# One-layer hybrid decoder step: the chunk's triangular inverse keeps its transposed copy by VectorE 32x32 transposes instead of TensorE products

## The chip, the cores and the metric

The kernel runs on one core of a Trainium2 chip, in one launch. The metric is the device time of that launch in microseconds (us). PE is TensorE, DVE is VectorE, ACT is ScalarE, POOL is GpSimd, and SP is SyncE, which only issues transfers here.

## What is computed

One layer of a decoder is applied to a prompt of 16 + 1024 rows and to 8 single-row samples: RMSNorm, an input projection, RWKV-7 time mixing beside forgetting attention, gates, an output projection and an MLP. The change lies inside the time mixing of the prompt. In the reference it is a recurrence over rows for each of 8 heads:

```python
def step(state, inp):
    r_t, w_t, k_t, v_t, kk_t, a_t = inp
    s_kk = jnp.einsum('bhvk,bhk->bhv', state, kk_t)
    state = (state * w_t[:, :, None, :]
             - s_kk[..., None] * (kk_t * a_t)[:, :, None, :]
             + v_t[..., None] * k_t[:, :, None, :])
    return state, jnp.einsum('bhvk,bhk->bhv', state, r_t)
```

The kernel computes it for 104 rows at a time (a chunk). Within a chunk the terms `s_kk` of later rows depend on earlier ones, which gives a unit triangular 104x104 system for each head, and its inverse is what the change touches.

## The kernel before

The 1040 prompt rows are 10 chunks (`c` = 0 to 9), which run one after the other; each engine has its own program for a chunk (`pe_chunk` L996, `act_chunk` L1532, `dve_chunk` L1884, the loop of POOL L2316), and they meet through counting semaphores. Each list `Steps` (L597 to L610) names an engine's steps in order, and `wait(steps, name)` waits for one of them.

**Fillers.** The chunk's own matrix products are small and depend on each other, so TensorE fills its waiting time with the next projection of the layer. A unit of it is 3 matmuls of 128x128 by 350 columns (L384 to L386; in chunk 0 one fp32 matmul, L388). A chunk has 48 units: 24 of weight tile 0, then 24 of weight tile 1. `fill.run(n)` puts n units at a fixed place of the program: 16 at the chunk's start, 4 among the first products, 4 ahead of the inverse (so that it begins with tile 1), 2 in each of levels 1 to 6, 4 behind, 8 at the end. The first unit of a tile waits until ScalarE has rounded its weights (`fill_split_high`) and VectorE has made the remainder (`fill_split_low`, L585 to L590, two instructions of 128x512 for tile 1).

**The inverse.** Heads lie as 8 blocks of columns; of the 104 rows, 64 are "top" and 40 "low", two separate triangles held in one tile at 64 columns a head. The inverse grows by levels: at level lv diagonal blocks of 2^lv are joined to blocks of twice the size by X <- X - X B X, with B the products masked for this level. X is kept as `Xm`, and its transpose as `XTr`, since a matmul wants its left operand transposed. Heads go in two halves, q = 0 and 1. `by_halves` (L1015) issues one head as two fp32 matmuls, 64x64 (L1020) and 40x40 (L1021); the profile shows each as two records. The steps are:

- POOL makes the mask products `bm_lv_top` (64x512) and `bm_lv_low` (40x320) at L2326 for levels 0 to 5, alternately in two buffers, from the step `mask_b1` on.
- VectorE, behind the mask products of L1913, does `fill_split_low` (L1918), waits for `bm_0_low` and makes `XTr` = I - B (`xt_init`, L1920).
- TensorE turns it into `Xm` (steps `x_0`, `x_1`, L1068 to L1071), and ScalarE copies that from PSUM (L1565 to L1567).
- In a level TensorE makes `t1` = B X (L1073 to L1082), ScalarE copies it (L1575), 2 filler units run, then TensorE makes `t2x` (L1084 to L1095) and `t2` (L1096 to L1099). VectorE subtracts `t2x` from `Xm` (L1934) and `t2` from `XTr` (L1940). The next `t1` waits for the first, the next `t2x` for the second.
- Level 5 puts its `XTr` part into `XTF` (L1943, L1945), and level 6 joins top and low (L1106, L1115, L1948).

```python
for q in range(2):
    for j in range(4):
        last = by_halves(4 + q, j, T1, XTr, 4 * q + j)
    ch_pe.done(last, f"t2_{lv}_{q}")
```

Of the kernel before, what the change touches and what calls it, by code (L numbers as in the profile page):

```python
# [41 lines left out]
P = 128  # L42
# [7 lines left out]
C = 104  # L50
NC = TP // C
HD = 64
NH = 8
# [12 lines left out]
C_LV = C_CM + 2 * C  # L66
N_LV = 7
# [64 lines left out]
def build(nc, A):  # L132
    with ExitStack() as ctx:
        def sem(name):
            return ctx.enter_context(nc.semaphore(name))
# [449 lines left out]
        def fill_split_low(dve, i, s):  # L585

            dve.wait_ge(wf_high[s], i)
            for k0, k1, t in WF[s]:
# [5 lines left out]
        LEVELS = range(1, N_LV)  # L594
        ch_pe = Steps(sem("ch_pe"), ["nat_k", "nat_b", "nat_v"]
                      + [f"prod_{m}{i}" for i in range(2) for m in "kb"] + ["z", "x_0", "x_1"]
                      + [f"{t}_{lv}_{q}" for lv in LEVELS for t in (("t1", "t2x", "t2") if lv < N_LV - 1 else ("t1", "t2"))  # L597
                         for q in range(2)]
                      + ["u", "y", "s", "yt"])
        ch_act = Steps(sem("ch_act"), ["v", "e1", "e3", "e2", "nat_k", "z", "x_0", "x_1"]  # L600
# [3 lines left out]
                       + [f"mask_{m}{i}" for i in range(2) for m in "kb"] + ["xt_init"]  # L604
# [5 lines left out]
        ch_pool = Steps(sem("ch_pool"), [f"bm_{lv}_{b}" for lv in range(N_LV - 1) for b in ("top", "low")] + ["bonus", "gate"])  # L610
# [279 lines left out]
        def _(pe):  # L890
# [105 lines left out]
            def pe_chunk(c):  # L996
                fill = Filler(pe, c + V_FOX0, NS, hl_made if c == 1 else None) if c else fill0

                def wait(steps, name):
                    pe.wait_ge(steps.sem, steps.after(c, name))  # L1000
# [66 lines left out]
                wait(ch_dve, "xt_init")  # L1067
                for q in range(2):  # L1068
                    for j in range(4):
                        last = by_halves(q, j, XTr, identP)  # L1070
                    ch_pe.done(last, f"x_{q}")  # L1071
                for lv in LEVELS[:-1]:
                    for q in range(2):  # L1073
                        if q == 0:
                            pe.wait_ge(ch_pool.sem, ch_pool.after(c, f"bm_{lv}_low"))
                        if lv == 1:
                            wait(ch_act, f"x_{q}")
                        else:
                            wait(ch_dve, f"x_{lv - 1}_{q}_x")
                        for j in range(4):  # L1080
                            last = by_halves(q, j, Bm[lv % 2], Xm, 4 * q + j)
                        ch_pe.done(last, f"t1_{lv}_{q}")  # L1082
                    fill.run(2)
                    for q in range(2):  # L1084
                        wait(ch_act, f"t1_{lv}_{q}")
                        if lv > 1:
                            wait(ch_dve, f"x_{lv - 1}_{q}_xt")
                        for j in range(4):
                            h = 4 * q + j
                            if lv < N_LV - 2:  # L1090
                                last = by_halves(2 + q, j, XTr, T1, h)
                            else:
                                last = pe.matmul(PS[top, 2 + q, j * HB:(j + 1) * HB], XTr[top, h], T1[top, h],
                                                 start=True, stop=True)
                        ch_pe.done(last, f"t2x_{lv}_{q}")  # L1095
                    for q in range(2):  # L1096
                        for j in range(4):
                            last = by_halves(4 + q, j, T1, XTr, 4 * q + j)
                        ch_pe.done(last, f"t2_{lv}_{q}")  # L1099
# [354 lines left out]
        def _(act):  # L1454
# [77 lines left out]
            def act_chunk(c, gates, early=True):  # L1532
# [32 lines left out]
                for q in range(2):  # L1565
                    wait(ch_pe, f"x_{q}")
                    ch_act.done(act.copy(quad(Xm, q), PS[0:C, q, 0:4 * HB]), f"x_{q}")  # L1567
                out(2)
                for lv in LEVELS:
                    for q in range(2):  # L1570
                        wait(ch_pe, f"t1_{lv}_{q}")
                        if lv > 1:
                            wait(ch_pe, f"t2_{lv - 1}_{q}")
                        part = slice(0, C) if lv < N_LV - 1 else low
                        ch_act.done(act.copy(quad(T1, q)[part], PS[part, q, 0:4 * HB]), f"t1_{lv}_{q}")  # L1575
# [210 lines left out]
        def _(dve):  # L1786
# [93 lines left out]
            order(dve.memset(XTF[low, :, top], 0.0))  # L1880
            order(dve.tensor_copy(identP[top], ident[top, 0:HB]))
            order(dve.tensor_copy(identP[low], ident[low, HB:2 * HB]))
            dve.sem_inc(ch_dve.sem, 1)
            def dve_chunk(c, early=True):  # L1884
# [25 lines left out]
                for i in range(2):  # L1910
                    for m, dst, bank in (("k", MK, 4), ("b", MB, 0)):
# [4 lines left out]
                            cm, ALU.mult), f"mask_{m}{i}")  # L1916
                if early:
                    fill_split_low(dve, c, 1)  # L1918
                wait(ch_pool, "bm_0_low")
                done(dve.tensor_tensor(XTr[0:C], identP[0:C].unsqueeze(1).to_broadcast([C, NH, HB]),  # L1920
                                       Bm[0][0:C], ALU.subtract), "xt_init")
# [4 lines left out]
                for lv in LEVELS:  # L1926
# [9 lines left out]
                    for q in range(2):  # L1936
                        wait(ch_pe, f"t2_{lv}_{q}")
                        four = slice(4 * q, 4 * q + 4)
                        if lv < N_LV - 2:
                            done(dve.tensor_tensor(quad(XTr, q), quad(XTr, q), PS[0:C, 4 + q, 0:4 * HB],  # L1940
                                                   ALU.subtract), f"x_{lv}_{q}_xt")
                        elif lv < N_LV - 1:
# [370 lines left out]
        def _(pool):  # L2313

            pool.sem_inc(ch_pool.sem, 1)
            with pool.Fori(0, NC) as c:  # L2316
                pool.wait_ge(ch_dve.sem, ch_dve.after(c, "mask_b1"))
                for lv in range(N_LV - 1):
                    if lv == 2:
                        pool.wait_ge(ch_dve.sem, ch_dve.after(c, "xt_init"))  # L2320
# [154 lines left out]
```

## Time and profile before

| | us |
|---|---|
| median of 3 runs (2086.79 to 2089.35) | 2087.89 |
| the profiled execution, its own time | 2083.8 |
| its span, first to last instruction | 2082.0 |
| PE busy in it | 2001.7 (96%) |
| DVE, ACT, POOL busy | 953.7, 631.4, 219.9 |

The ten chunks begin at 232.6, 300.6, 358.3, 415.8, 473.3, 530.8, 588.2, 645.7, 703.2 and 760.7 us of the span, and the last one's own products end at 806.2. Times in the rows are counted from the start of the span. Chunk 5 (530.76 to 588.24) stands for chunks 1 to 9, which repeat to 0.3 us.

### The profile page before, as it was taken

Reading aid. Unit: us, or ns where it says so; the run is one execution under the profiler, and the core shown is the slowest. Engines: PE = TensorE matmul, PEld = TensorE weight load, DVE = VectorE, ACT = ScalarE, POOL = GpSimd, SP = SyncE. Lnnn points to the kernel's source line nnn. Section 1 sums busy time; section 2 is a strip of 40 time slices with the busy share of each in tenths; the row PEclk is TensorE's granted clock in tenths of the full one; section 3 lists DMA queues with packets and bytes.
Section 4 is the critical chain, followed back from the end, with each engine's and each line's share of the span. In section 5 each row is a group of like instructions: output and inputs, shape, how many; then the busy total and the mean of one; then the engine's idle time right before and its main releaser. Section 6 shows DMA issues by size and latency. Waiting matters only on the chain.

```text
span 2082.0 us, 43790 instructions
## 1 busy us (share of the span) xinstructions
PE 2001.7 (96%) x18026; PEld 1864.0 (90%) x18026; DVE 953.7 (46%) x1509; ACT 631.4 (30%) x1011; POOL 219.9 (11%) x197
## 2 busy tenths in 40 slices
PE   7999999999999998798998999999999999999997
PEld 7997679999999998785666999999999999999997
DVE  6556564445555554417786654332132223222324
ACT  5114333322333333135455543321022012102313
POOL 0000212323333321121110000000000000000000
PEclk9999999999999999999999999999999999999998
DMA  4213721122223213657643741111111111111112
GB/s 172 90 32 137 241 48 41 42 59 50 60 70 80 80 55 94 178 189 240 236 162 138 243 146 41 51 41 51 41 50 41 51 40 50 40 50 41 50 41 83
DMA packets 111982, 189.65 MB, mean 91 GB/s; under 512 B 62870, under 2 KB 66230, under 8 KB 110406
## 3 DMA queue, kind: packets, MB, share of 16 engines
q1 hardware_dynamic: 109542, 179.15, 27.5%
q10 hardware_dynamic: 2304, 8.50, 1.3%
q8 instruction: 109, 1.79, 0.4%
q14 instruction: 27, 0.22, 0.0%
HBM read 149.83 MB, written 37.79 MB: 90 GB/s over the span
## 4 chain that ended last, share of the span: by engine, by line
PE 52%; issue 31%; POOL 7%; DMA 3%; DVE 3%; SPq 2%; ACT 1%; POOLq 0%; ACTq 0%; DVEq 0%
PE ps L294 44%; POOL arena L2326 6%; PE ps L384 1%; DMA weights<-in_wu 1%; PE ps L385 1%; PE ps L386 1%; SPq L811 1%; SPq L817 1%; DMA normed<-in_vp 1%; DMA normed<-in_kp 1%; PE ps L1272 1%; PE ps L1213 1%; DVE arena L2085 1%; DVE arena L2104 1%; POOL arena L2332 1%
## 5 line engine op out<-in xcount | busy, mean ns | idle before, releaser
L294 PE MATMUL ps<-h_high,wb_split 128*128 128x350 f32 (+1 forms) x1536 | 290.6, 324 | 0.0
L294 PE MATMUL ps<-ff_high,wb_split 128*128 128x350 f32 x1488 | 280.2, 323 | 0.0
L304 ACT CAST wb_split<-weights 128x1024 fp32r<-128x1024 f32 x88 | 92.2, 1047 | 592.9 <-PE ps L294 592.9
L294 PEld LDWEIGHTS ps<-h_high,wb_split 128*128 128x128 f32 x1536 | 254.5, 189 | 0.4
L294 PEld LDWEIGHTS ps<-ff_high,wb_split 128*128 128x128 f32 x1488 | 246.7, 189 | 0.0
L2243 DVE TENSOR_TENSOR arena<-arena,ps 128x1050 f32 (+1 forms) x39 | 48.7, 1249 | 311.1 <-PE ps L294 311.1
L2326 POOL TENSOR_TENSOR arena<-arena,constants 64x512 f32<-64x512 f32 x120 | 140.6, 1172 | 357.7 <-DVE arena L1913 322.4
L1020 PEld LDWEIGHTS ps<-arena 64*64 64x64 f32 x2400 | 145.0, 135 | 21.2 <-issue 10.0
L1020 PE MATMUL ps<-arena 64*64 64x64 f32 x2400 | 154.0, 219 | 7.6 <-POOL arena L2326 7.5
L294 PE MATMUL ps<-ff_low,wb_split 128*128 128x350 f32 x744 | 160.6, 324 | 0.0
L386 PE MATMUL ps<-fill_high,w_fill_low 128*128 128x350 f32 x468 | 152.9, 327 | 0.0
L1021 PE MATMUL ps<-arena 40*40 40x64 f32 x2400 | 149.6, 218 | 0.0
L2260 DVE SCALAR_TENSOR_TENSOR squares<-ps,arena 128x1050 f32<-128x1050 f32 x32 | 40.1, 1252 | 220.2 <-PE ps L294 209.8
L1021 PEld LDWEIGHTS ps<-arena 40*40 40x40 f32 x2400 | 138.7, 112 | 0.0
L294 PEld LDWEIGHTS ps<-ff_low,wb_split 128*128 128x128 f32 x744 | 127.0, 189 | 0.0
L294 PE MATMUL ps<-h_high,w_split 128*128 128x350 f32 (+1 forms) x576 | 115.2, 332 | 2.9 <-DVE w_split L308 2.9
L308 DVE TENSOR_TENSOR wb_split<-weights,wb_split 128x1024 fp32r<-128x1024 f32 x88 | 107.3, 1219 | 2.3 <-DVE fox L2222 1.8
L1934 DVE TENSOR_TENSOR arena<-arena,ps 104x256 f32<-104x256 f32 (+1 forms) x100 | 42.0, 420 | 142.7 <-PE ps L1021 117.6
L385 PE MATMUL ps<-fill_low,w_fill 128*128 128x350 f32 x312 | 103.2, 331 | 0.0
L294 PEld LDWEIGHTS ps<-h_high,w_split 128*128 128x128 f32 x576 | 97.5, 191 | 5.7 <-DVE w_split L308 3.2
L384 PE MATMUL ps<-fill_high,w_fill 128*128 128x350 f32 x234 | 82.7, 353 | 12.3 <-POOL w_fill_low L589 9.0
L386 PEld LDWEIGHTS ps<-fill_high,w_fill_low 128*128 128x128 f32 x468 | 90.1, 193 | 0.0
(346 smaller groups left out, 3672.0 us busy)
## 6 DMA issues: line engine op xcount, KB each, us to landing
weights<-in_wu SPq DMA_DIRECT2D x122, 512.0 KB, 3.7
normed<-in_vp SPq DMA_DIRECT2D x64, 260.0 KB, 4.7
normed<-in_kp SPq DMA_DIRECT2D x64, 256.0 KB, 4.6
arena<-chunk_dram SPq DMA_DIRECT2D x10, 1248.0 KB, 6.9
arena<-gate_dram SPq DMA_DIRECT2D x16, 525.0 KB, 4.2
chunk_dram<-arena SPq DMA_DIRECT2D x12, 520.0 KB, 5.0
chunk_dram<-fox SPq DMA_DIRECT2D x12, 520.0 KB, 4.6
arena<-samp_dram SPq DMA_DIRECT2D x10, 512.0 KB, 10.1
```

What stands on the lines that cost most here:

```text
L294: last = pe.matmul(PS[:, 3 * s + g, 0:n], ws[s][wh][:, k * P:(k + 1) * P], tile_of(x[xh], k)[:, g * G:g * G + n], start=(k == 0 and wh + x ...
L304: act.copy(of[0][s][0], W[:, s]).then_inc(w_hi[s], 1)
L308: dve.tensor_tensor(of[0][s][1], W[:, s], of[0][s][0], ALU.subtract).then_inc(w_split[s], 1)
L384: self.pe.matmul(out, fill_w(s, k), HF[k][:, at], start=(i == 0), stop=False)
L385: self.pe.matmul(out, fill_w(s, k), HL[:, k, at], start=False, stop=False)
L386: last = self.pe.matmul(out, wl_, HF[k][:, at], start=False, stop=(i == KT - 1))
L1020: pe.matmul(PS[top, bank, at], a[top], b[top], start=True, stop=True)
L1021: return pe.matmul(PS[low, bank, at], a[low, 0:HR], b[low], start=True, stop=True)
L1934: done(dve.tensor_tensor(quad(Xm, q)[part], quad(Xm, q)[part], PS[part, 2 + q, 0:4 * HB], ALU.subtract), f"x_{lv}_{q}_x")
L2243: dve.tensor_tensor(dst, dst, grp(s), ALU.add).then_inc(evac[s], 1)
L2260: dve.scalar_tensor_tensor(g3(RL[s]), grp(s), 0.0, rstd1, ALU.max, ALU.mult)\
L2326: ch_pool.done(pool.tensor_tensor(Bm[lv % 2][part, :, 0:n], MB[part, :, 0, part], mask.unsqueeze(1).to_broadcast([n, NH, n]), ALU.mult), f ...
```

## The change

The transposed copy `XTr` is no longer made by products up to block size 32: VectorE turns 32x32 blocks of `Xm` into it (`blocks_turned`), which is enough while X has no entries outside diagonal blocks of 32. The product `t2` is left for level 5 (and 6). The start works the other way round: VectorE makes the level-0 mask product itself (two instructions), then `XTr`, then `Xm` by one transpose of 128x512, so that the steps `x_0` and `x_1` of TensorE and ScalarE are gone. `fill_split_low` comes behind that. POOL begins with level 1. The fillers of levels 1 to 5 are 0, 3, 2, 3, 2 units instead of 2 each, the same 10 in all. ScalarE's copy of `t1` waits for `t2x` of the level before. Two more memsets stand ahead of chunk 0.

```diff
--- before.py
+++ after.py
@@ -592,22 +592,24 @@
         bonus_added = sem("bonus_added")
 
         LEVELS = range(1, N_LV)
+        IN_LEVEL = (0, 3, 2, 3, 2)
         ch_pe = Steps(sem("ch_pe"), ["nat_k", "nat_b", "nat_v"]
-                      + [f"prod_{m}{i}" for i in range(2) for m in "kb"] + ["z", "x_0", "x_1"]
-                      + [f"{t}_{lv}_{q}" for lv in LEVELS for t in (("t1", "t2x", "t2") if lv < N_LV - 1 else ("t1", "t2"))
+                      + [f"prod_{m}{i}" for i in range(2) for m in "kb"] + ["z"]
+                      + [f"{t}_{lv}_{q}" for lv in LEVELS for t in ("t1", *(("t2x",) if lv < N_LV - 1 else ()),
+                                                                    *(("t2",) if lv >= N_LV - 2 else ()))
                          for q in range(2)]
                       + ["u", "y", "s", "yt"])
-        ch_act = Steps(sem("ch_act"), ["v", "e1", "e3", "e2", "nat_k", "z", "x_0", "x_1"]
+        ch_act = Steps(sem("ch_act"), ["v", "e1", "e3", "e2", "nat_k", "z"]
                        + [f"t1_{lv}_{q}" for lv in LEVELS for q in range(2)]
                        + ["nu", "ln", "rstd"] + [f"y_{p}" for p in range(HP)])
         ch_dve = Steps(sem("ch_dve"), [f"scan_{p}" for p in range(HP)] + ["lm", "r", "k", "b", "a", "nat_b", "nat_v"]
-                       + [f"mask_{m}{i}" for i in range(2) for m in "kb"] + ["xt_init"]
+                       + [f"mask_{m}{i}" for i in range(2) for m in "kb"] + ["bm_0_top", "bm_0_low", "xt_init", "x_init"]
                        + [f"x_{lv}_{q}_{t}" for lv in LEVELS
                           for t, q in (([("x", 0), ("x", 1)] if lv < N_LV - 1 else [])
                                        + [(t, q) for q in range(2)
                                           for t in (("xt", "xl") if lv == N_LV - 2 else ("xt",))])]
                        + ["sum", "mean", "state_sum", "state", "center", "sq", "var", "norm"])
-        ch_pool = Steps(sem("ch_pool"), [f"bm_{lv}_{b}" for lv in range(N_LV - 1) for b in ("top", "low")] + ["bonus", "gate"])
+        ch_pool = Steps(sem("ch_pool"), [f"bm_{lv}_{b}" for lv in LEVELS[:-1] for b in ("top", "low")] + ["bonus", "gate"])
 
         ds_pe, ds_act, ds_dve = sem("ds_pe"), sem("ds_act"), sem("ds_dve")
         ds_store, ds_load = sem("ds_store"), sem("ds_load")
@@ -1064,23 +1066,18 @@
                                      skip_group_check=True)
                 ch_pe.done(last, "z")
                 fill.run(4)
-                wait(ch_dve, "xt_init")
-                for q in range(2):
-                    for j in range(4):
-                        last = by_halves(q, j, XTr, identP)
-                    ch_pe.done(last, f"x_{q}")
+                wait(ch_dve, "x_init")
                 for lv in LEVELS[:-1]:
                     for q in range(2):
                         if q == 0:
                             pe.wait_ge(ch_pool.sem, ch_pool.after(c, f"bm_{lv}_low"))
-                        if lv == 1:
-                            wait(ch_act, f"x_{q}")
-                        else:
+                        if lv > 1:
                             wait(ch_dve, f"x_{lv - 1}_{q}_x")
                         for j in range(4):
                             last = by_halves(q, j, Bm[lv % 2], Xm, 4 * q + j)
                         ch_pe.done(last, f"t1_{lv}_{q}")
-                    fill.run(2)
+                    if IN_LEVEL[lv - 1]:
+                        fill.run(IN_LEVEL[lv - 1])
                     for q in range(2):
                         wait(ch_act, f"t1_{lv}_{q}")
                         if lv > 1:
@@ -1093,10 +1090,10 @@
                                 last = pe.matmul(PS[top, 2 + q, j * HB:(j + 1) * HB], XTr[top, h], T1[top, h],
                                                  start=True, stop=True)
                         ch_pe.done(last, f"t2x_{lv}_{q}")
-                    for q in range(2):
-                        for j in range(4):
-                            last = by_halves(4 + q, j, T1, XTr, 4 * q + j)
-                        ch_pe.done(last, f"t2_{lv}_{q}")
+                for q in range(2):
+                    for j in range(4):
+                        last = by_halves(4 + q, j, T1, XTr, 4 * q + j)
+                    ch_pe.done(last, f"t2_{N_LV - 2}_{q}")
 
                 lv = N_LV - 1
                 for q in range(2):
@@ -1562,15 +1559,12 @@
                 def quad(ap, q):
                     return ap[0:C, 4 * q:4 * q + 4].rearrange("p a b -> p (a b)")
 
-                for q in range(2):
-                    wait(ch_pe, f"x_{q}")
-                    ch_act.done(act.copy(quad(Xm, q), PS[0:C, q, 0:4 * HB]), f"x_{q}")
                 out(2)
                 for lv in LEVELS:
                     for q in range(2):
                         wait(ch_pe, f"t1_{lv}_{q}")
                         if lv > 1:
-                            wait(ch_pe, f"t2_{lv - 1}_{q}")
+                            wait(ch_pe, f"{'t2x' if lv < N_LV - 1 else 't2'}_{lv - 1}_{q}")
                         part = slice(0, C) if lv < N_LV - 1 else low
                         ch_act.done(act.copy(quad(T1, q)[part], PS[part, q, 0:4 * HB]), f"t1_{lv}_{q}")
                     if lv == 4:
@@ -1878,6 +1872,8 @@
             for b in Bm:
                 order(dve.memset(b[low, :, HR:HB], 0.0))
             order(dve.memset(XTF[low, :, top], 0.0))
+            order(dve.memset(XTr, 0.0))
+            order(dve.memset(Xm[96:P], 0.0))
             order(dve.tensor_copy(identP[top], ident[top, 0:HB]))
             order(dve.tensor_copy(identP[low], ident[low, HB:2 * HB]))
             dve.sem_inc(ch_dve.sem, 1)
@@ -1914,11 +1910,20 @@
                             dst[0:C].rearrange("p (e a) x t -> p e a (x t)", e=2)[:, :, 2 * i:2 * i + 2],
                             PS[0:C, bank:bank + 2, 0:4 * C].rearrange("p e (a n) -> p e a n", a=2),
                             cm, ALU.mult), f"mask_{m}{i}")
+                for part, name in ((top, "top"), (low, "low")):
+                    n = part.stop - part.start
+                    mask = cst[part, C_LV + part.start:C_LV + part.stop]
+                    done(dve.tensor_tensor(XTr[part, :, 0:n], MB[part, :, 0, part],
+                                           mask.unsqueeze(1).to_broadcast([n, NH, n]), ALU.mult), f"bm_0_{name}")
+                done(dve.tensor_tensor(XTr[0:C], identP[0:C].unsqueeze(1).to_broadcast([C, NH, HB]),
+                                       XTr[0:C], ALU.subtract), "xt_init")
+
+                def blocks_turned(dst, src):
+                    return dve.transpose(dst.rearrange("p a b -> p (a b)"), src.rearrange("p a b -> p (a b)"))
+
+                done(blocks_turned(Xm, XTr), "x_init")
                 if early:
                     fill_split_low(dve, c, 1)
-                wait(ch_pool, "bm_0_low")
-                done(dve.tensor_tensor(XTr[0:C], identP[0:C].unsqueeze(1).to_broadcast([C, NH, HB]),
-                                       Bm[0][0:C], ALU.subtract), "xt_init")
 
                 def quad(ap, q):
                     return ap[0:C, 4 * q:4 * q + 4].rearrange("p a b -> p (a b)")
@@ -1934,12 +1939,12 @@
                             done(dve.tensor_tensor(quad(Xm, q)[part], quad(Xm, q)[part], PS[part, 2 + q, 0:4 * HB],
                                                    ALU.subtract), f"x_{lv}_{q}_x")
                     for q in range(2):
-                        wait(ch_pe, f"t2_{lv}_{q}")
                         four = slice(4 * q, 4 * q + 4)
                         if lv < N_LV - 2:
-                            done(dve.tensor_tensor(quad(XTr, q), quad(XTr, q), PS[0:C, 4 + q, 0:4 * HB],
-                                                   ALU.subtract), f"x_{lv}_{q}_xt")
-                        elif lv < N_LV - 1:
+                            done(blocks_turned(XTr[:, four], Xm[:, four]), f"x_{lv}_{q}_xt")
+                            continue
+                        wait(ch_pe, f"t2_{lv}_{q}")
+                        if lv < N_LV - 1:
                             done(dve.tensor_tensor(XTF[top, four, top], XTr[top, four], moved(4 + q, top, HB),
                                                    ALU.subtract), f"x_{lv}_{q}_xt")
                             done(dve.tensor_tensor(XTF[low, four, low], XTr[low, four, 0:HR], moved(4 + q, low, HR),
@@ -2315,9 +2320,7 @@
             pool.sem_inc(ch_pool.sem, 1)
             with pool.Fori(0, NC) as c:
                 pool.wait_ge(ch_dve.sem, ch_dve.after(c, "mask_b1"))
-                for lv in range(N_LV - 1):
-                    if lv == 2:
-                        pool.wait_ge(ch_dve.sem, ch_dve.after(c, "xt_init"))
+                for lv in LEVELS[:-1]:
                     if lv > 2:
                         pool.wait_ge(ch_pe.sem, ch_pe.after(c, f"t1_{lv - 2}_1"))
                     for part, name in ((top, "top"), (low, "low")):
```

## Rows read from the trace of the kernel before

**Rows 1.** Page: busy time, and the PE and clock lines of 40 slices

```profile
PE 2001.7 (96%) x18026; PEld 1864.0 (90%) x18026; DVE 953.7 (46%) x1509; ACT 631.4 (30%) x1011; POOL 219.9 (11%) x197
...
PE   7999999999999998798998999999999999999997
...
PEclk9999999999999999999999999999999999999998
```

**Rows 2.** Stages of chunk 5: busy time, granted clock, DMA share, GB/s

```profile
core 0: us, PE busy (x) PEld busy (x) DVE busy (x) ACT busy (x) POOL busy (x), PEclk, DMA share, GB/s
546.29:550.38 4.09, 4.09 (x103) 3.81 (x102) 1.69 (x4) 0.74 (x2) 3.19 (x4) 1.00 0.24 34
...
542.00:546.29 4.29, 3.45 (x71) 2.95 (x70) 0.00 (x0) 1.84 (x5) 3.98 (x4) 1.00 0.09 8
...
530.76:588.24 57.48, 56.64 (x850) 53.04 (x849) 29.78 (x52) 17.61 (x38) 16.48 (x14) 1.00 0.22 54
```

**Rows 3.** Timeline of PE in chunk 5: start, us, instruction, [idle before <-releaser]

```profile
542.08 0.27 PE L1020 MATMUL ps<-arena 64*64 64x64 f32 x1
...
544.07 0.27 PE L1020 MATMUL ps<-arena 64*64 64x64 f32 x1 [0.84 <-POOL arena L2326]
...
545.14 0.43 PE L384 MATMUL ps<-fill_high_b,w_fill1b 128*128 128x350 f32 x1
...
546.29 0.27 PE L1020 MATMUL ps<-arena 64*64 64x64 f32 x1
...
549.23 0.43 PE L384 MATMUL ps<-fill_high,w_fill1b 128*128 128x350 f32 x1
...
562.66 0.27 PE L1093 MATMUL ps<-arena 64*64 64x64 f32 x1
```

**Rows 4.** Timeline of ACT and DVE in level 1 of chunk 5

```profile
544.79 0.37 ACT L1575 COPY arena<-ps 104x256 f32<-104x256 f32 x1 [0.80 <-PE ps L1021]
...
547.09 0.42 DVE L1934 TENSOR_TENSOR arena<-arena,ps 104x256 f32<-104x256 f32 x1 [5.15 <-PE ps L1021]
```

**Rows 5.** Timeline of DVE ahead of the inverse of chunk 5

```profile
535.98 2.08 DVE L1913 TENSOR_TENSOR arena<-ps,constants 104x832 f32<-104x832 f32 x2 [0.55 <-PE ps L1051]
538.10 0.69 DVE L589 TENSOR_TENSOR w_fill_low<-weights,w_fill1a 128x512 fp32r<-128x512 f32 x1
538.71 1.76 DVE L589 TENSOR_TENSOR w_fill_low<-weights,w_fill1b 128x512 fp32r<-128x512 f32 x1
541.25 0.69 DVE L1920 TENSOR_TENSOR arena<-arena 104x512 f32<-104x512 f32 x1 [0.79 <-POOL arena L2326]
```

**Rows 6.** Timeline of POOL there: levels 0 and 1, and level 2's first

```profile
538.14 1.77 POOL L2326 TENSOR_TENSOR arena<-arena,constants 64x512 f32<-64x512 f32 x1 [8.99 <-DVE arena L1913]
539.99 1.23 POOL L2326 TENSOR_TENSOR arena<-arena,constants 40x320 f32<-40x320 f32 x1
541.29 1.78 POOL L2326 TENSOR_TENSOR arena<-arena,constants 64x512 f32<-64x512 f32 x1
543.15 0.86 POOL L2326 TENSOR_TENSOR arena<-arena,constants 40x320 f32<-40x320 f32 x1
544.17 1.26 POOL L2326 TENSOR_TENSOR arena<-arena,constants 64x512 f32<-64x512 f32 x1 [0.16 <-POOL arena L2326]
```

**Rows 7.** Groups by line over the ten chunks, PE

```profile
L1020 PE MATMUL ps<-arena 64*64 64x64 f32 x2400 | 154.0, 219 | 7.6 <-POOL arena L2326 7.5
L1021 PE MATMUL ps<-arena 40*40 40x64 f32 x2400 | 149.6, 218 | 0.0
```

**Rows 8.** Timeline of DVE ahead of chunk 0

```profile
225.82 0.27 DVE L1877 MEMSET arena<- 128x256 f32 x1 [0.17 <-DVE arena L1860]
...
226.90 0.48 DVE L1880 MEMSET arena<- 40x512 f32 x1 [0.17 <-DVE arena L1879]
...
229.05 1.60 DVE L1895 TENSOR_TENSOR_SCAN arena<-constants,arena 128x104 f32<-128x104 f32 x4 [1.22 <-DMA arena<-chunk_dram]
```

**Rows 9.** Waits of chunks 1 to 9: engine, line, releaser: us in total, times, longest

```profile
DVE arena L1895 <- PE ps L993: 6.3, 8, 0.8
```

## The prediction

> **What bounds the kernel now.** I read the page first: TensorE is busy 96% of the span and its clock is granted at full speed (2.4 GHz) in nearly every slice [rows 1]. The change lies only in the ten chunks, so the next view is the table of stages. In chunk 5, TensorE is busy 56.64 of 57.48 us, DVE 29.78, ACT 17.61, POOL 16.48, and the DMA share is 0.22 [rows 2]. A busy TensorE that runs small dependent products may still be waiting inside, so I looked at the timeline: records follow each other without a gap, except 0.84 us in front of level 1, which POOL's mask product ends [rows 3]. Over all chunks these gaps are 7.5 us [rows 7]. So a chunk lasts as long as TensorE's own program, and a product that goes away is worth its time, unless something that it covered becomes visible. DVE's next chunk begins when TensorE releases it, not when a DMA does [rows 9], so no transfer sets the period. 0.2% of the time, 4.2 us, is about what a measurement of this kernel can tell from no change.
>
> **The removed products.** From 546.29 to 549.23 TensorE does three product steps of 8 heads (t2x, t2 and the next t1), then turns to a filler [rows 3]. From 544.07 to 545.14 it does one, 1.07 us. Two more steps cost 2.94 - 1.07 = 1.87, so a step is 0.94 us and the turn to a filler 0.13. The four t2 of levels 1 to 4 are 4 x 0.94 = **3.76 us** a chunk. One block of fillers fewer (level 1 has none; the units are the same) saves one turn, **0.13**. The step from the first product x_0 to level 1's first product lasts 544.07 - 542.08 = **1.99 us**, its wait for POOL and its ScalarE copies within it, and all of it goes. As a check on the count: 40 of 120 heads' products of L1020 and L1021 a chunk go, which in [rows 7] is 800 of 2400 records on each line.
>
> **What comes in place of the x steps.** DVE now makes Xm before level 1 may start. Its mask products end at 535.98 + 2.08 = 538.06 [rows 5]. Then come the top mask product (64x512: by L1920's 512 columns, 0.69), the low one (40x320), xt_init (0.69) and the transpose of 512 columns, while POOL starts level 1's masks at 538.14 as before. They get in each other's way. The second L589 takes 1.76 against 0.69 for the first, and it ends 0.56 after POOL's first product at 539.91; POOL's 64x512 takes 1.77 and 1.78 beside DVE and 1.26 alone [rows 5, 6]. So each stands still until the other's instruction ends, and then needs 0.56 (DVE, 512 columns), 1.13 (POOL, 512) or 0.75 (POOL, 320: 540.47 to 541.22). Walked through: top to 538.79; POOL to 539.91; low to 540.27 (320 of 512 columns of 0.56); POOL to 541.02, which is level 1's mask, long before need; xt_init to 541.58; the transpose to 542.31 if it costs 0.69; released after 0.06, which is what POOL's end at 543.15 + 0.86 = 544.01 needs to reach TensorE at 544.07 [rows 3, 6]. TensorE arrives at 542.08 and so waits **0.29 us**.
>
> The rows don't show either whether a transpose beside POOL stands still. In the walk POOL would be in level 2's top product until 542.71, and a transpose that waits for it ends at 543.27, 0.96 later than I have it. The rows show a block only between two operations that both read two SBUF tensors, while L1934, with one operand in SBUF and one in PSUM, costs its 0.42 in a stage where POOL is busy for 3.19 of 4.09 us [rows 2, 4]. So I take the free one. The Trainium skill ("SBUF — State Buffer", section Who interferes with whom) says that only VectorE operations with two SBUF inputs, or in a two-port mode, exclude GpSimd, and lists fp32 copies, but not transposes, among the latter. By the first half of that rule the sum would stay; if a transpose counts as a copy, it would lose 10 us over the chunks.
>
> **Level 1.** t1 is followed at once by t2x, which needs ScalarE's copy: it ends 544.79 + 0.37 - 544.07 = 1.09 after t1's start [rows 4], plus 0.06 release is 1.15, against 0.94 of work: **0.21 lost**. Then DVE has fill_split_low in front of the x update. By the same walk its halves end at 543.27 (behind POOL's top product) and 544.58 (behind its low one), while the update is wanted at 542.37 + 1.15 + 0.80 = 544.32 (0.80 is t2x's start to DVE's start, 546.29 to 547.09 [rows 3, 4]): **0.30 lost**. The filler that needs the split comes in level 2, behind the next t1, at about 546.1, so it doesn't wait. Without a filler in level 1 that cover is not missed either.
>
> **The turnaround.** Before, t2 ran while DVE updated Xm. Now the next t1 follows t2x. It can start at 0.80 + 0.42 + 0.06 = 1.28 after t2x's start, against 0.94 of work: 0.34 lost in each of four levels, **1.36 us**. Half q = 1 is just in time (0.46 later, like the products). A transpose of XTr costs TensorE nothing: in a level with two filler units it has from the Xm updates' end (0.41 after t1's start) until t1 and the fillers are over, 1.07 + 1.15 - 0.41 = 1.8 us for the first half (1.15 is the two fillers, 545.14 to 546.29) and 0.47 more for the second, against 0.42 and 0.84. POOL's masks lie a level ahead and start earlier than before. ScalarE has two copies less. The memsets ahead of chunk 0 (about 0.5 each, [rows 8]) fit in the 1.22 us that DVE waits there for its DMA. Loads of weights hang on the same units as before and have whole levels of time.
>
> **The sum.** 3.76 + 0.13 + 1.99 - 0.29 - 0.21 - 0.30 - 1.36 = 3.72 us a chunk, 37 us for ten (chunk 0 has no split behind x_init, but other fillers; I count it alike). What follows the chunks hangs on TensorE too and moves up as a whole. Against the profiled execution's 2083.8 that gives 2047; the median of the runs lies 4 us above it, so I say **2051**.
>
> **Rivals.**
> 1. *Dearer hand-overs* (0.07). Each new wait of TensorE is a two-engine hand-over, priced above from waits that were hidden. If x_init is late by 1.3 more (a dear transpose that also waits for POOL) and each of five hand-overs costs 0.25 more, 1.2 us a chunk is left: 2076. For it: DVE and POOL do collide there [rows 5, 6]. Against: the 0.06 of the one visible release.
> 2. *Slower: the transposes are so slow that TensorE waits for them in each level* (0.04). With a cost of T for 256 columns, x_init takes 2T, and the second half's transpose is late in the levels with two fillers from T = 1.1, with three from T = 1.3. The losses eat up the 3.72 at about T = 1.4, 3.3 times an L1934; at T = 1.8 a chunk is 4 us longer and the time is 2127. Against it: nothing on DVE costs over half of that per column.
> 3. *Nothing becomes visible* (0.05): DVE and ScalarE answer within the running half, and the whole 5.9 us of a chunk go: 2029. Against it: 0.80 and 0.42 are measured and t1 can't start without Xm.
> 4. *The time is not TensorE's* (0.03): the chunk's period is held by a transfer or by DVE's own chain, and what is saved comes back as a wait at the chunk's start: no change, 2088. Against it: [rows 2, 9].
> That the short waits lower the clock is no rival with a price: the stage with the 0.84 us gap has a granted clock of 1.00 [rows 2].
>
> **How the numbers follow.** The forecast has 0.81. Its own bounds: without collisions and without the split's delay a chunk saves 4.3, with a turnaround also 0.1 shorter 4.7, so 2040; with the transpose blocked (0.96) or dear, and hand-overs 0.1 dearer, it saves about 2.2, so 2066. The four rivals, 0.19, lie outside. Faster by over 0.2% are the forecast and rivals 1 and 3: 0.93; no change 0.03; slower 0.04.
>
> **What would show it.** In the profile after: L1020 with 1600 records instead of 2400; chunk periods of 53.8 instead of 57.48; a wait of about 0.3 in front of level 1 with DVE's transpose as releaser and none by POOL; gaps of about 0.34 in front of t1 in levels 2 to 5, released by L1934, with somewhat more in level 2; transposes of 0.42 (256 columns) and 0.69 (512). Gaps in front of t2x in levels 2 to 5 would speak for rival 2, a gap at a chunk's start for rival 4. I am wrong in the mechanism if the period shrinks by less than 2 us while the gaps are as small as I say.

## The result, and the profile after

Four runs of the changed kernel have a median of 2051.8 us (2047.5 to 2055.8), four of the kernel before 2087.3 (2085.7 to 2089.4): ratio of the two 0.9831, 95% interval 0.9811 to 0.9851. The forecast was 2051, within 2040 to 2066. The profiled execution took 2047.5 us against 2083.8.

The page of the changed kernel, its head, its clock line, and the groups of the two lines of 8-head products (before: [rows 1, 7]; L1022 and L1023 are the old L1020 and L1021, L1939 the old L1934, L2329 the old L2326, and L1922 is the transpose):

```profile
span 2045.6 us, 40598 instructions
...
PE 1963.2 (96%) x16426; PEld 1820.4 (89%) x16426; DVE 987.8 (48%) x1541; ACT 625.9 (31%) x991; POOL 202.3 (10%) x177
...
PEclk9999999999999998999999999999999999999999
...
L1022 PE MATMUL ps<-arena 64*64 64x64 f32 x1600 | 113.0, 220 | 9.7 <-DVE arena L1939 5.3
...
L1023 PE MATMUL ps<-arena 40*40 40x64 f32 x1600 | 109.2, 218 | 0.0
```

800 records have gone from each line, TensorE is busy 38.5 us less and VectorE 34.1 more, and the wait in front of the products is now VectorE's work, not POOL's. The idle total that is printed there has hardly grown (9.7 us against 7.6).

The table of stages for chunk 5, first the whole chunk, then level 1 to level 2's t1, then level 2's t2x to level 3's. The columns are those of [rows 2]: stretch, length, busy time of PE, PEld (loading of weights), DVE, ACT and POOL, granted clock, DMA share and GB/s.

```profile
512.23:565.78 53.55, 52.60 (x689) 48.63 (x688) 33.09 (x55) 16.99 (x36) 14.58 (x12) 1.00 0.23 58
523.84:526.48 2.64, 2.28 (x65) 2.03 (x65) 2.52 (x4) 1.19 (x3) 2.40 (x3) 1.00 0.10 5
529.18:532.69 3.51, 3.35 (x71) 2.96 (x70) 1.74 (x4) 0.74 (x2) 2.21 (x3) 1.00 0.43 149
```

A chunk lasts 53.55 us in place of 57.48, 3.93 less; chunks 2 to 8 agree to 0.06 us, chunk 1 went from 57.72 to 53.76 and chunk 0 from 68.01 to 64.56. The timeline of TensorE there (before: [rows 3]):

```profile
523.84 0.27 PE L1022 MATMUL ps<-arena 64*64 64x64 f32 x1
...
526.48 0.24 PE L1022 MATMUL ps<-arena 64*64 64x64 f32 x1 [0.35 <-DVE arena L1939]
...
529.18 0.27 PE L1022 MATMUL ps<-arena 64*64 64x64 f32 x1
...
530.47 0.24 PE L1022 MATMUL ps<-arena 64*64 64x64 f32 x1 [0.15 <-POOL arena L2329]
...
540.20 0.27 PE L1090 MATMUL ps<-arena 64*64 64x64 f32 x1
```

Counted from the chunk's start, level 1 begins at 523.84 - 512.23 = 11.61 (before 13.31) and level 5's t2x at 27.97 (before 31.90). From level 2's t2x at 529.18 to the next t1 it is 1.29. The idle time printed there is only 0.15, because it is counted from the modelled end of the last product; the start-to-start time is what a level pays. POOL is named as its releaser, but its mask for this level had ended at 528.1; what ended at 530.47 is the next level's. VectorE's L1939, over at 530.33, is what TensorE waited for.

In front of level 1 the PE timeline prints no idle time, but the one of the weight loads does, with VectorE's transpose as the releaser:

```profile
523.83 0.13 PEld L1022 LDWEIGHTS ps<-arena 64*64 64x64 f32 x1 [0.41 <-DVE arena L1922]
```

The fillers in front of level 1 begin at 9.28 of the chunk (before 9.21) and take 2.11 where nothing waits behind them, so TensorE arrives at 11.39 and waits 0.22.

The timeline of VectorE ahead of the inverse, and POOL's instructions at the time of xt_init and of the transpose (before: [rows 5, 6]):

```profile
519.58 2.16 DVE L1916 TENSOR_TENSOR arena<-arena,constants 64x512 f32<-64x512 f32 x2
521.78 1.25 DVE L1918 TENSOR_TENSOR arena<-arena 104x512 f32<-104x512 f32 x1
523.07 0.71 DVE L1922 STREAM_TRANSPOSE arena<-arena 128x512 f32<-128x512 f32 x1
523.82 0.91 DVE L589 TENSOR_TENSOR w_fill_low<-weights,w_fill1a 128x512 fp32r<-128x512 f32 x1
524.65 1.35 DVE L589 TENSOR_TENSOR w_fill_low<-weights,w_fill1b 128x512 fp32r<-128x512 f32 x1
525.93 0.95 DVE L1939 TENSOR_TENSOR arena<-arena,ps 104x256 f32<-104x256 f32 x2
526.91 0.93 DVE L1922 STREAM_TRANSPOSE arena<-arena 128x256 f32<-128x256 f32 x2
```

```profile
521.47 1.01 POOL L2329 TENSOR_TENSOR arena<-arena,constants 40x320 f32<-40x320 f32 x1
522.56 1.61 POOL L2329 TENSOR_TENSOR arena<-arena,constants 64x512 f32<-64x512 f32 x1
```

xt_init (L1918) costs 1.25 in place of 0.69 because POOL holds it up, as walked through: it ends 0.55 after POOL's 40x320. The transpose from 523.07 runs its 0.71 in the middle of a POOL instruction (522.56 to 524.17) and isn't held up. Nor is any other, by the view of its line (the durations are the shortest, the median and the longest in ns), though 40 of the 90 overlap an instruction of POOL:

```profile
L1922 DVE STREAM_TRANSPOSE arena<-arena x90: 445/445/712, 244.6 to 753.2; 128x256 f32<-128x256 f32 x80, 128x512 f32<-128x512 f32 x10
```

### The profile page after: what moved, and what is told of

The parts are those of the page before. It is cut to its first block, busy times and chain, and to the rows that moved or that the text cites. A ratio compares the mean times of both kernels' runs of the same rounds, so it can differ in the third digit from the quotient of the medians.

```text
span 2045.6 us, 40598 instructions
## 1 busy us (share of the span) xinstructions
PE 1963.2 (96%) x16426; PEld 1820.4 (89%) x16426; DVE 987.8 (48%) x1541; ACT 625.9 (31%) x991; POOL 202.3 (10%) x177
## 4 chain that ended last, share of the span: by engine, by line
PE 53%; issue 31%; POOL 7%; DVE 3%; DMA 2%; SPq 2%; ACT 1%; POOLq 0%; ACTq 0%; DVEq 0%
PE ps L294 44%; POOL arena L2329 6%; PE ps L384 1%; PE ps L386 1%; PE ps L385 1%; SPq L819 1%; DMA normed<-in_vp 1%; POOL w_fill_low L589 1%; PE ps L1210 1%; DMA weights<-in_wu 1%; DMA normed<-in_kp 1%; PE ps L1269 1%; DVE arena L2109 1%; DVE arena L2090 1%; PE ps L1314 1%
## 5 line engine op out<-in xcount | busy, mean ns | idle before, releaser
L2329 POOL TENSOR_TENSOR arena<-arena,constants 64x512 f32<-64x512 f32 x100 | 122.0, 1220 | 344.7 <-DVE arena L1909 323.2
L1022 PEld LDWEIGHTS ps<-arena 64*64 64x64 f32 x1600 | 101.0, 134 | 25.9 <-issue 17.0
L1022 PE MATMUL ps<-arena 64*64 64x64 f32 x1600 | 113.0, 220 | 9.7 <-DVE arena L1939 5.3
L1023 PE MATMUL ps<-arena 40*40 40x64 f32 x1600 | 109.2, 218 | 0.0
L1023 PEld LDWEIGHTS ps<-arena 40*40 40x40 f32 x1600 | 93.6, 112 | 0.0
L2090 DVE CUSTOM_DVE_ANT_0 arena<-ps,arena 104x416 f32<-104x416 f32 (+3 forms) x152 | 68.1, 494 | 31.8 <-PE ps L1314 31.7
```

The lines of the kernel that those rows point to most:

```text
L1022: pe.matmul(PS[top, bank, at], a[top], b[top], start=True, stop=True)
L1023: return pe.matmul(PS[low, bank, at], a[low, 0:HR], b[low], start=True, stop=True)
L2090: dve.tensor_tensor_reduce(Sm[u % 3][0:C, e, lo:hi].rearrange("p b t -> p (b t)"), PS[0:C, 2 * (n % 2) + e, (lo - CUTS[c][0]) * C:(hi - CU ...
L2329: ch_pool.done(pool.tensor_tensor(Bm[lv % 2][part, :, 0:n], MB[part, :, 0, part], mask.unsqueeze(1).to_broadcast([n, NH, n]), ALU.mult), f ...
```

## The experiments

Where the outcome is a chunk period, it is that of chunk 5 in the table of stages.

**The changed kernel again.** 

> The changed kernel once more, in more rounds beside the kernel before, since its four runs lay 8 us apart. If the chunks alone carry the change, the ratio is 0.982 to 0.984 (2083.8 less 36 us) and the chunk period is again 53.55 us. If part of it was chance in the stages behind the chunks, where the two profiled executions differ by 1.3 us of waits, the ratio moves by up to 0.001 with the same period.

Median 2051.0 (five runs), ratio 0.9835, interval 0.9813 to 0.9858; period 53.54. The ratio holds. The runs still spread over 6 us. From the last product of the last chunk to the end it took 1276.1 us in the profile of before, 1277.7 in that of the changed kernel and 1281.2 in this one, with nothing changed there: this spread comes from the stages behind the chunks, so below the periods decide, which repeat to some 0.03 us.

**Only the levels.** Made from the kernel before: the start as it was, two fillers in each level. ScalarE's copy of `t1` waits for `t2x`, and the two memsets are there, as in the changed kernel.

```diff
-                    for q in range(2):
-                        for j in range(4):
-                            last = by_halves(4 + q, j, T1, XTr, 4 * q + j)
-                        ch_pe.done(last, f"t2_{lv}_{q}")
+                for q in range(2):
+                    for j in range(4):
+                        last = by_halves(4 + q, j, T1, XTr, 4 * q + j)
+                    ch_pe.done(last, f"t2_{N_LV - 2}_{q}")
...
-                            done(dve.tensor_tensor(quad(XTr, q), quad(XTr, q), PS[0:C, 4 + q, 0:4 * HB],
-                                                   ALU.subtract), f"x_{lv}_{q}_xt")
+                            done(blocks_turned(XTr[:, four], Xm[:, four]), f"x_{lv}_{q}_xt")
```

> Only the levels are changed: XTr by transposes in levels 1 to 4; the start (POOL's level-0 mask, x_0 and x_1 by TensorE) and two filler units in each level as before. Theory (a chunk lasts as long as TensorE's program): four steps of 0.94 us less, four turnarounds of 0.34 more, 2.40 us a chunk: period 55.1, 24 us in all, ratio 0.9885. Rival (the t2 products only filled time in which TensorE waits for Xm, and the gain sits in the start): under 1 us a chunk, period 56.5 or more, ratio 0.995 or more.

```profile
518.98:574.18 55.20, 53.81 (x722) 49.62 (x721) 29.94 (x52) 17.61 (x38) 16.48 (x14) 1.00 0.22 56
```

2.28 us a chunk less (2.40 expected), ratio 0.9893 (0.9867 to 0.9919). The rival falls: the four t2 steps were worth their time less the turnaround. The wait for POOL in front of level 1 stays, 0.77 here.

**Only the start.** Made from the changed kernel: t2 is a product in all levels, TensorE makes it within each level, and ScalarE's copy waits for it again.

```diff
-                            done(blocks_turned(XTr[:, four], Xm[:, four]), f"x_{lv}_{q}_xt")
-                            continue
+                            done(dve.tensor_tensor(quad(XTr, q), quad(XTr, q), PS[0:C, 4 + q, 0:4 * HB],
+                                                   ALU.subtract), f"x_{lv}_{q}_xt")
```

> Only the start is changed: VectorE makes the level-0 mask product, XTr and, by one transpose, Xm; t2 is a TensorE product again in all levels; fillers 0, 3, 2, 3, 2 as in the changed kernel. Theory: 1.70 us less up to level 1, 0.21 lost in front of level 1's t2x, 0.13 for a filler block less: 1.6 us a chunk, period 55.9, 16 us, ratio 0.992. Together with the levels alone this should make the whole, 3.9 us. Rival (the gain sits in the start): 3 us or more a chunk, period 54.5, ratio 0.986.

```profile
521.85:577.57 55.72, 55.58 (x818) 52.05 (x816) 32.88 (x55) 16.96 (x36) 14.56 (x12) 1.00 0.23 56
```

1.76 us a chunk less (1.70 - 0.21 + 0.13 = 1.62 expected), ratio 0.9918 (0.9893 to 0.9942). The parts add up within 0.11: 2.28 + 1.76 = 4.04 against 3.93 for both. Only in the whole does TensorE wait for an update of Xm that stands behind fill_split_low, about 0.2 (1.49 from level 1's t2x to level 2's t1 against 1.30 in the later levels).

**Even fillers.** `IN_LEVEL = (2, 2, 2, 2, 2)` in the changed kernel. 

> The changed kernel with two filler units in each of levels 1 to 5, as before the change. Theory: level 1's first unit is of weight tile 1 and waits for fill_split_low, which VectorE now ends 13.8 us after the chunk's start (12.7 would be in time), so level 1 grows and levels 2 and 4 shrink by a unit each: 1.0 us a chunk more than the changed kernel, period 54.6, with a gap of about 1.1 in front of level 1's filler. Rival (the order of the fillers is of no account, TensorE is busy anyway): period 53.5 to 53.7.

```profile
518.20:572.83 54.63, 52.80 (x689) 48.62 (x688) 33.19 (x55) 16.96 (x36) 14.54 (x12) 1.00 0.22 57
```

The timeline of TensorE has the gap where it was expected:

```profile
532.03 0.43 PE L384 MATMUL ps<-fill_high_b,w_fill1b 128*128 128x350 f32 x1 [1.07 <-DVE w_fill_low L589]
```

So moving level 1's fillers away is a needed part of the change, worth 1.08 us a chunk once fill_split_low comes late (ratio 0.9892).

**The split first.** In the changed kernel `fill_split_low(dve, c, 1)` moves from behind x_init to ahead of the level-0 mask product. 

> The changed kernel with fill_split_low back in its old place, ahead of VectorE's level-0 mask product. Theory (POOL and VectorE block each other for whole instructions when both read two SBUF tensors): x_init is there at 14.6 us of the chunk in place of 11.5, level 2 no longer waits for VectorE, period 56.3. Rival (no blocking, only VectorE's own 2.4 us of split and less): the split would cost 1.3 us at most, since without blocking its halves take 0.69 each: period 54.9 or less.

x_init came when the blocking says it does: TensorE starts at 14.57 us of the chunk (14.6 expected). Here is VectorE in chunk 5 behind the split (the level-0 mask product in its two instructions, xt_init, the transpose), and the first product of level 1:

```profile
540.15 2.85 DVE L1918 TENSOR_TENSOR arena<-arena,constants 64x512 f32<-64x512 f32 x2
543.03 1.24 DVE L1920 TENSOR_TENSOR arena<-arena 104x512 f32<-104x512 f32 x1
544.30 0.71 DVE L1924 STREAM_TRANSPOSE arena<-arena 128x512 f32<-128x512 f32 x1
```

```profile
545.07 0.27 PE L1022 MATMUL ps<-arena 64*64 64x64 f32 x1 [3.08 <-DVE arena L1924]
```

But the periods are 57.3 to 59.8, not 56.3, and the ratio is 1.0014 (1.0000 to 1.0029). The stages of chunk 6: the wait for x_init, the products of level 1 to level 2's t1, the three fillers, and what follows:

```profile
600.00:602.57 2.57, 0.00 (x1) 0.00 (x1) 2.44 (x3) 0.00 (x0) 1.14 (x2) 0.78 0.12 7
602.57:607.95 5.38, 5.38 (x97) 5.26 (x97) 1.74 (x4) 1.12 (x3) 2.12 (x2) 0.50 0.60 173
607.95:611.00 3.05, 3.05 (x13) 2.67 (x15) 0.00 (x0) 0.37 (x1) 2.13 (x2) 0.50 0.13 54
611.00:616.00 5.00, 4.69 (x103) 4.19 (x101) 2.18 (x6) 0.75 (x2) 2.14 (x2) 0.93 0.01 3
```

After the wait of 3.1 us the granted clock is 0.50, the lower of its two levels (1.2 GHz), and the three product steps of level 1 and level 2's t1 last 5.3 us (to 607.88). They take 3.7 in the changed kernel, and 3.5 at full clock where nothing waits for the split (the next run). The fillers take 2.9 in place of 1.6. The period of this chunk is 59.81; in chunk 5 the mean clock was 0.70 and 0.79 in these stages and the period 57.50.

**The split first, with cover.** Eight fillers in front of the inverse in place of four, and 0, 1, 1, 2, 2 in the levels. 

> The kernel with fill_split_low ahead of the level-0 mask product again, but with 8 filler units in front of the inverse in place of 4 and 0, 1, 1, 2, 2 in the levels. Theory (in the run with the split first the wait of 3.1 us for x_init lowered TensorE's clock behind it, which made 56.3 into 57.3 to 59.8): the wait shrinks to 1.2 us, the clock stays at full, and the period is 56.3 less the four units of 0.48 that move into the wait: 54.4, the same in all chunks. Rival (the split's old place delays something else in the levels by 1 to 3.5 us): the period stays 1 us or more above 54.4 and uneven.

```profile
514.74:569.14 54.40, 52.59 (x690) 48.61 (x689) 33.99 (x55) 17.00 (x36) 14.30 (x12) 1.00 0.23 57
```

It is 54.40 to 54.47 in chunks 2 to 8 (54.64 in chunk 1, which is 0.2 longer in the kernels before and after the change too); the wait is 1.17 and the clock stays at 1.00. So it was the clock, lowered behind the longer wait, and not the place of the split. Ratio 0.9885.

**The level transposes twice.** Each is made a second time under a step of its own and writes the same. 

> The changed kernel with each transpose of XTr in levels 1 to 4 made twice (the second writes the same). Theory: it has some 0.85 us of slack in front of each t2x, so 0.48 and 0.96 more on VectorE cost at most 0.1 us a level: period 53.55 to 53.7. Rival (transposes stand on the path): at least 0.45 a level, period 55.4 or more.

```profile
511.40:564.97 53.57, 52.62 (x691) 48.64 (x689) 36.64 (x63) 16.98 (x36) 14.56 (x12) 1.00 0.23 58
```

VectorE works 3.55 us more and the chunk is as long as before (ratio 0.9838). The transposes of XTr are not on the path.

**The first transpose twice.** 

> The changed kernel with the transpose of 128x512 that makes Xm done twice. Theory: it stands on the path, 0.75 us more in front of level 1, of which about 0.2 comes back in level 2, since the split is then over before the update of Xm is due: period 54.1 to 54.3, a gap of 0.8 to 0.9 in front of level 1. Rival (x_init is covered by the fillers in front of it): period within 0.1 of 53.55.

```profile
515.01:569.10 54.09, 52.58 (x690) 48.62 (x688) 33.37 (x56) 16.98 (x36) 14.27 (x12) 1.00 0.23 57
```

TensorE's wait in front of level 1, in the timeline:

```profile
527.37 0.27 PE L1022 MATMUL ps<-arena 64*64 64x64 f32 x1 [0.87 <-DVE arena L1922]
```

Of 0.75 us, 0.54 stays; the rest comes back in level 2, where t1 now starts 2.45 after level 1's start instead of 2.64 (ratio 0.9870). x_init is on the path.

**One filler unit between t2x and t1.**

```diff
-        IN_LEVEL = (0, 3, 2, 3, 2)
+        IN_LEVEL = (0, 2, 1, 2, 1)
...
                         ch_pe.done(last, f"t2x_{lv}_{q}")
+                    if lv < N_LV - 2:
+                        fill.run(1)
```

> The changed kernel with one filler unit between t2x and the next t1 in levels 1 to 4, and fillers 0, 2, 1, 2, 1 between t1 and t2x: the same units in all. Theory: the next t1 starts at 0.94 + 0.13 + 0.48 = 1.55 after t2x's start in place of 1.28, but 0.48 of filler is gone elsewhere, so a level costs 0.21 less, 0.84 a chunk: period 52.7, 8 us faster than the changed kernel, no gap in front of t1. Rival (the waits of 0.15 to 0.35 that the profile shows in front of t1 are all there is to win, and each more turn to a filler costs as much): period 53.4 to 53.7, no gain.

A miss for the theory: the period is 53.30, 0.25 less, though the gaps in front of t1 are gone. The timeline of TensorE at level 2's t2x, its one unit, and level 3's t1:

```profile
527.08 0.27 PE L1022 MATMUL ps<-arena 64*64 64x64 f32 x1
...
528.16 0.43 PE L384 MATMUL ps<-fill_high,w_fill1b 128*128 128x350 f32 x1
528.43 0.32 PE L385 MATMUL ps<-fill_low,w_fill1b 128*128 128x350 f32 x1
528.59 0.32 PE L386 MATMUL ps<-fill_high,w_fill_low 128*128 128x350 f32 x1
528.84 0.27 PE L1022 MATMUL ps<-arena 64*64 64x64 f32 x1
```

The unit takes 0.68, not 0.48: besides the 0.14 in front of it, 0.20 go within and behind it, since the second matmul starts 0.27 after the first and the next small product 0.25 after the third, where in a run of fillers it is 0.16 from start to start. These 0.20 come once a block and not once a unit: blocks of 1, 2, 3 and 10 units last 0.68, 1.16, 1.64 and 5.01 in these kernels. A block of fillers costs 0.33 beside its units, nearly as much as the wait that it covers (1.76 - 0.48 = 1.28 against 1.29). Only in level 1, where the wait was longer (2.64 - 1.15 = 1.49), is 0.2 gained. That was the term I had too small. The median was 2046.1, ratio 0.9817 (0.9794 to 0.9839) beside 0.9835 (0.9813 to 0.9858) in the same session; the times alone don't tell the two apart.

**One block.** All ten units behind level 1's t2x, none in levels 2 to 5. 

> The changed kernel with all ten filler units of levels 1 to 5 in one block behind t2x of level 1, and none elsewhere in them. Theory, corrected by the run with one unit between t2x and t1: a block of fillers costs a fixed 0.33 us beside its units (0.13 to turn to it, 0.20 to turn back), against 0.21 lost where t2x waits for ScalarE without one and 0.35 where t1 waits for VectorE. So levels 2 to 5 save 0.11 each, level 1's turn 0.23: period 52.9, 6 us faster than the changed kernel. The transposes of XTr then end 0.1 to 0.2 before t2x wants them. Rival (fillers within the levels cover the transposes and POOL's masks): gaps in front of t2x or behind POOL, period 54 or more.

```profile
508.81:561.95 53.14, 52.27 (x689) 48.73 (x688) 33.08 (x55) 16.89 (x36) 14.55 (x12) 1.00 0.23 58
```

53.14, 0.41 less than the changed kernel, where 0.67 was expected: fillers within the levels cover nothing that matters, so the rival falls. But a level without them runs 1.23 from t1 to t2x in level 2 (527.65 to 528.88) and 1.20 in levels 3 to 5, and not 1.15 as in level 1, so that levels 2 to 5 gain about 0.05 each and not 0.11. What makes the 0.05 to 0.08 I can't say; in level 2 ScalarE's copy begins 0.80 after t1, in level 1 0.73. By the period, ten chunks are 4 us shorter than in the changed kernel; the median is 2048.5, ratio 0.9830 (0.9815 to 0.9845), which doesn't show it.

## Why the prediction was right

It was right in its mechanism and in most terms, one was mis-sized by more than half, and some small errors cancelled; each step can be held against a row.

- **What bounds it.** Right: each part alone takes its own share off, a chunk shortens by TensorE's removed work less new waits, and VectorE's doubled level transposes cost nothing.
- **Removed products.** 3.76 and 1.99 a chunk: the start went from 13.31 to 11.61, which is the predicted 1.99 - 0.29 to the hundredth. VectorE sets this moment; the wait itself was 0.22 and not 0.29, since TensorE arrived 0.07 later than before, for a reason that the runs leave open. The blocking walk gave that: its times for xt_init's end (521.78 + 1.25 = 523.03, which is 10.80 of the chunk; predicted 541.58 - 530.76 = 10.82) hold within 0.03 us.
- **The transpose.** Taken at 0.69 and 0.42, measured 0.71 and 0.45. The side argument that a transpose of 256 columns stays under 0.75 was worked out wrongly: it doubled the bf16 figure of the Trainium skill ("VectorE: DVE Perf Modes", section The three transpose paths) once, but 256 columns of fp32 are four times the bytes of 128 columns of bf16. Four times the figure, as an estimate, is above 0.75, so by bytes it bounds nothing; the sum didn't use it. That it runs free beside POOL was a choice between two values; the row from 523.07 decides it. This agrees with what the Trainium skill says ("SBUF — State Buffer", section Who interferes with whom) of operations with one SBUF input outside the two-port modes, and puts the fp32 transpose on the side of the unblocked.
- **Level 1.** t2x starts 1.15 after t1 as predicted; t1 of level 2 at 1.49 after that, predicted 1.58, since VectorE began the update of Xm at 13.70 of the chunk and not at 13.86.
- **The turnaround.** 1.28 predicted; 1.29 to 1.30 measured in front of levels 3, 4 and 5, and in front of level 2 as well once the split is over in time (the first transpose twice); in the changed kernel that one is the 1.49 above. Two of its parts are off and cancel: VectorE begins its update (0.42 long) 0.73 after t2x and not 0.80 (529.91 against 529.18), and from its end at 530.33 to TensorE's next t1 at 530.47 it is 0.14, not the 0.06 seen behind POOL and again behind x_init.
- **One term was mis-sized**: "one block of fillers fewer saves one turn, 0.13". It saves 0.33, as the run with one unit between t2x and t1 showed. I had the turn to the filler from two rows and had left the rest, 0.20, inside the units' price (1.15 for two). It is also most of the 0.14 by which the start alone beat its expectation.
- **The sum again**, with what was measured: start 1.70, four t2 steps of 0.934 or 3.74, one block of fillers fewer 0.33, less 0.22 for level 1's t2x, 0.19 for the split and 4 x 0.36 for the turnarounds, makes 3.92 of the 3.93. Against the predicted 3.72, the block gave 0.20 more and the split cost 0.11 less, and the turnarounds cost 0.08 more.
- **The memsets** ahead of chunk 0 were said to fit in a wait of 1.22 us. They cost 0.3 once: each took 0.48 and the 0.17 in front of it, 1.30 in all, and 0.22 of idle time still stands in front of the scan. The time from the first product of L981 (L983 in the changed kernel), in the stage before, to chunk 0's first product grew from 21.39 to 21.70.
- **The total** fitted better than its parts deserve: the chunks gave 38.6 us and not 37, the start of the span and the stages behind the chunks took 2.3 back in this pair of profiles, within the spread of the latter.

Of the rivals, dearer hand-overs and slow transposes are refuted by the rows above; that nothing becomes visible is refuted by the 1.29; that the time isn't TensorE's by the parts that add up. But I set the clock aside too easily. "The stage with the 0.84 us gap has a granted clock of 1.00" was true and enough for this change, whose waits are 0.1 to 0.35. It said nothing about a wait of 3.1 us, and there the clock fell to half and cost 1.0 to 3.5 us a chunk more than the 56.3 that was expected without it. With x_init 3 us late, as in the run with the split first, the change is no gain at all.

## What to carry to other kernels

Where TensorE fills its waits with other work, price a removed product at its full start-to-start time, then subtract for each hand-over that it covered the difference between the hand-over's length and the work left beside it; idle time as printed understates this. Price each switch between kinds of matmul both ways before adding more, smaller fillers. An operation moved to a second engine shifts what stands behind it in that engine's queue: here the place of level 1's fillers decided 1.1 us a chunk, and the place of the split 3.7 to 6.3, the clock included, as much as the products themselves.

## What the runs showed of the hardware

- The VectorE 32x32 transpose in fp32 costs 0.445 us for 128x256 and 0.71 for 128x512 (from the two, an estimate of 1.04 ns a column and 0.18 fixed), and it is not held up by a GpSimd operation beside it, while xt_init with its two SBUF inputs took 1.25 in place of 0.69.
- A block of 350-column fillers among 64-column fp32 products costs TensorE 0.33 us beside its own matmuls, whatever its length: 0.14 in front of it, 0.11 behind its first matmul, 0.09 behind its last.
- Behind a wait of 3.1 us the granted clock of TensorE fell to its lower level: its mean was 0.50 in the 8.4 us that followed in chunk 6, and 0.70 and 0.79 in the stages of the 6.3 us that followed in chunk 5. Small products of 3.5 us at full clock took 5.3 in chunk 6. Behind waits of 1.1 us (even fillers) and 1.2 (the split first, with cover) it stayed at 1.00.
